# A hybrid attention and recurrence backbone: three kinds of work that surround the projections are moved, and the two edge query blocks of each head are scored in 512 columns

## The reference, cut to what matters

```python
for l in range(DEPTH):                                   # DEPTH = 2
    sh1, sc1, g1, sh2, sc2, g2 = adaln(c, mod_w[l], mod_b[l])   # silu(c) @ mod_w[l] + mod_b[l], six vectors
    n_lat = modulate(rmsnorm(h, norm1_g[l]), sh1, sc1)
    if even:  # one projection: q, k, v, xr, gr = split(n_lat @ w_in); the context gives k, v, xr too
        y = concat(neighbourhood_attention(q, k, v, kc, vc, rpb), bidir_rglru(...) * gelu(gr)) @ w_out
    else:
        y = short_conv_mixer(n_lat, o_w_in[o], o_conv_w[o], o_w_out[o])
    h = h + g1 * y
    h = h + g2 * swiglu(modulate(rmsnorm(h, norm2_g[l]), sh2, sc2), ffn_w_gu[l], ffn_w_down[l])
return rmsnorm(h, final_g)
```

## Time and profile before

| what | value |
|---|---|
| time, median of 3 runs | 2314.98 us (2313.59 to 2317.13) |
| the profiled execution's own time | 2308.03 us |
| its span, first to last instruction | 2306.2 us |
| mean granted TensorE clock | 0.992 |
| PE busy | 2241.3 us, 97% |
| DVE busy | 1480.3 us, 64% |
| POOL busy | 1143.6 us, 50% |
| ACT busy | 839.7 us, 36% |
| DMA queue q1 (SP's), q10 (ACT's) | 257.61 MB and 21.50 MB |

### The profile page before, as it was taken

How to read it: one execution, slowest core, us unless ns; L and a number is a source line. 1 busy time by engine, 2 the same in 40 slices (tenths; PEclk the granted TensorE clock), 3 DMA queues, 4 the chain that set the end, 5 groups by cost and what they waited for, 6 DMA issues and landing times.

```text
span 2306.2 us, 27368 instructions
## 1 busy us (share of the span) xinstructions
PE 2241.3 (97%) x10278; PEld 1830.8 (79%) x10278; DVE 1480.3 (64%) x1895; ACT 839.7 (36%) x1395; POOL 1143.6 (50%) x729
## 2 busy tenths in 40 slices
PE   8999999989999999999999999999999999999998
PEld 3788887878778888888888778888788888888887
DVE  5677755853786555557776987765976555555553
ACT  4544545852533333332122622234433333332112
POOL 3223313788646555556353445574356555565340
PEclk9999999999999999999999999999999999999999
DMA  9655657744222222248653122250222222242321
GB/s 339 208 151 169 188 154 189 163 134 123 61 86 88 84 85 86 84 133 284 222 194 112 32 82 82 74 186 29 60 86 85 83 85 84 83 160 96 110 81 75
DMA packets 296943, 282.95 MB, mean 123 GB/s; under 512 B 64784, under 2 KB 242156, under 8 KB 296300
## 3 DMA queue, kind: packets, MB, share of 16 engines
q1 hardware_dynamic: 258747, 257.61, 36.0%
q10 hardware_dynamic: 37488, 21.50, 3.2%
q0 software_dynamic: 576, 2.10, 0.2%
HBM read 226.36 MB, written 57.16 MB: 123 GB/s over the span
## 4 chain that ended last, share of the span: by engine, by line
PE 68%; DVE 6%; POOL 2%; issue 1%; ACT 1%; DMA 1%; DVEq 0%; POOLq 0%; ACTq 0%
PE bank L1103 22%; PE bank L1105 22%; PE bank L1104 22%; DVE act_lo L2115 1%; DMA pair_raw<-in_ffn_w_gu 1%; DVE act_hi L2115 1%; POOL slot_lo L1064 1%; POOL slot L1064 1%; DVE x_rms L2107 0%; DVE pair_raw L2092 0%; PE bank L1138 0%; DMA pair_raw<-in_o_w_in 0%; DVE bank L2026 0%; DVE t_sum L2082 0%; DVE pair_raw L2085 0%
## 5 line engine op out<-in xcount | busy, mean ns | idle before, releaser
L2034 DVE SCALAR_TENSOR_TENSOR h<-bank,mods,h 128x512 f32<-128x512 f32 x384 | 287.7, 750 | 271.5 <-PE bank L1105 266.3
L1064 POOL TENSOR_TENSOR slot_lo<-pair_raw,slot_hi 128x512 fp32r<-128x512 f32 x112 | 170.5, 1522 | 293.7 <-ACT slot_hi L1601 293.7
L1064 POOL TENSOR_TENSOR slot<-pair_raw,slot 128x512 fp32r<-128x512 f32 x144 | 234.2, 1647 | 17.3 <-ACT slot L1601 17.3
L1064 POOL TENSOR_TENSOR slot_lo<-t_sum,slot_hi 128x512 fp32r<-128x512 f32 x109 | 162.7, 1514 | 146.3 <-ACT slot_hi L1601 146.3
L2195 DVE TENSOR_TENSOR bank<-bank,p 128x512 f32<-128x512 f32 x53 | 37.0, 698 | 284.5 <-PE bank L1105 284.4
L1601 ACT CAST slot_hi<-pair_raw 128x512 fp32r<-128x512 f32 x112 | 69.0, 616 | 301.6 <-DMA pair_raw<-in_ffn_w_gu 244.2
L1103 PE MATMUL bank<-act_lo,slot_hi 128*128 128x512 f32 x436 | 171.2, 393 | 6.5 <-DVE act_lo L2115 5.9
L1103 PE MATMUL bank<-a,slot_hi 128*128 128x512 f32 x436 | 171.8, 394 | 2.6 <-ACT p L1610 0.8
L1105 PE MATMUL bank<-a,slot_hi 128*128 128x512 f32 x436 | 170.5, 391 | 0.0
L1105 PE MATMUL bank<-act_lo,slot_hi 128*128 128x512 f32 x436 | 170.2, 390 | 0.0
L1104 PE MATMUL bank<-act_lo,slot_lo 128*128 128x512 f32 x436 | 170.2, 390 | 0.0
(11 more groups left out here) (320 smaller groups left out, 5985.8 us busy)
## 6 DMA issues: line engine op xcount, KB each, us to landing
pair_raw<-in_ffn_w_gu SPq DMA_DIRECT2D x88, 512.0 KB, 4.6
mod_in_f<-in_mod_w SPq DMA_DIRECT2D x48, 512.0 KB, 3.8
z_spill<-silu_g SPq DMA_DIRECT2D x88, 256.0 KB, 2.2
mod_in_p<-in_mod_w SPq DMA_DIRECT2D x32, 512.0 KB, 6.0
pair_raw<-in_o_w_in SPq DMA_DIRECT2D x24, 512.0 KB, 3.8
raw<-in_e_w_in SPq DMA_DIRECT2D x20, 512.0 KB, 5.2
low_f<-z_spill SPq DMA_DIRECT2D x40, 256.0 KB, 4.9
a_f<-z_spill SPq DMA_DIRECT2D x18, 512.0 KB, 5.8
```

The costliest lines, as they stand in the source:

```text
L1064: nc.gpsimd.tensor_tensor(low, from_, high, ALU.subtract).then_inc(s_wlo, 1)
L2034: V.scalar_tensor_tensor(out=dst, in0=bank[:, b, :], scalar=mods[:, gate, m:m + 1], in1=dst, op0=ALU.mult, op1=ALU.add).then_inc(s_hup, 1)
```

## The change

The edge blocks of a head (kind 0 and 1, the first and the last) have two key tiles and so 256 window and 256 context keys. They are now scored by two matmuls of 512 columns into bank 0 instead of four of 256 columns across banks 0 and 1; the bias tile, the source of `logits` and the order in `turn_probs` follow. The fills of the bias move ahead of the gate weights' loads, the widening and placing one round forward, four slice loads a round move behind the bias. The totals of vector i-2 are made one by one inside group 0 of `project_in(i)` (and for the third vector inside the second V tile). DVE adds the last four slices of a vector after `gate_low(i + 1)`. The last block of y is scaled by DVE, copied by ACT and subtracted by DVE.

```diff
@@ sync
             for j in range(2):
                 load_unit(4 + j, j, column_unit(w_in, P + order_p[j]))
+            fill_bias()
             sp.wait_ge(s_gwz, 1)
...
                 load_unit(4 * i + 2, 0, column_unit(w_in, i * P + order_p[2]))
-                if i >= 2:
+                load_unit(4 * i + 3, 1, column_unit(w_in, i * P + order_p[3]))
+                if i == 1:
+                    widen_bias()
+                else:
+                    place_bias(range(ROWS // 2 * (i - 2), ROWS // 2 * (i - 1)))
                     for k in range(4):
                         load_mod_p(i - 1, k)
-                load_unit(4 * i + 3, 1, column_unit(w_in, i * P + order_p[3]))
-                if i == 1:
-                    fill_bias()
-                elif i == 2:
-                    widen_bias()
-                else:
-                    place_bias(range(ROWS // 2))
...
-                    place_bias(range(ROWS // 2, ROWS))
-                if j == 2:
-                    for k in range(4):
-                        load_mod_p(LT - 1, k)
-            for k in range(4, FT):
+            for k in range(FT):
                 load_mod_p(LT - 1, k)
@@ gpsimd (far_rows is now filled at the start)
             def out_weight(j):
+                if j == 3:
+                    pool.wait_ge(s_yf, BLOCKS)
...
             for g in range(BLOCKS):
-                y_ready(g)
+                if g < BLOCKS - 1:
+                    y_ready(g)
+                if g == BLOCKS - 2:
+                    pool.sem_inc(s_preset, 1)
@@ tensor
+            def mod_total(n, acc, m):
+                if m == 0:
+                    pe.wait_ge(s_macc, 8 * n + 10)
+                mm = pe.matmul(bank[:, 7, m:m + 1], acc[:, m * P:(m + 1) * P], ones[:, 0:1], start=True, stop=True)
+                if m == FT - 1:
+                    mm.then_inc(s_mfin, 1)
... in project_in
+                    if i >= 2 and g == 0:
+                        pe.wait_ge(s_gatev, 12 * i + 3)
+                        totals = {k: (lambda k=k: mod_total(i - 2, mod_acc_p, k)) for k in range(FT)}
-                    if i and g == 9:
-                        pe.wait_ge(s_gatev, 12 * i + 3)
-                        mod_totals(i - 1, mod_acc_p)
... in scores
+                if kind(b) < 2:
+                    step = k0 // CTX
+                    both = [k.rearrange("p (a n) -> p a n", n=CTX)[:, 0:step + 1:step, :] for k in (kh, kl)]
+                    out_ = bank_f[:, 0:HALF].rearrange("p (a n) -> p a n", n=CTX)
+                    pe.matmul(out_, q, both[0], start=True, stop=False)
+                    mm = pe.matmul(out_, q, both[1], start=False, stop=True)
@@ scalar, after the attention
+            act.wait_ge(s_yf, BLOCKS)
+            nc.scalar.copy(block_of(BLOCKS - 1, act_hi), block_of(BLOCKS - 1, y_f)).then_inc(s_yh, 1)
@@ vector
... in recur
+                if i:
+                    mod_set(i - 1, i + 1)
                 for k in range(4):
                     mod_part(i, k)
...
-                for k in range(4, FT):
-                    mod_part(i, k)
...
                     gate_low(i + 1)
-                mod_set(i, i + 2)
+                for k in range(4, FT):
+                    mod_part(i, k)
... after the attention
+            dve.wait_ge(s_preset, 4)
+            dve.wait_ge(s_fold, BLOCKS)
+            dve.wait_ge(s_invr, BLOCKS)
+            V.tensor_tensor(last_y, last_y, inv_rows[...], ALU.mult).then_inc(s_yf, 1)
+            dve.wait_ge(s_yh, BLOCKS)
+            V.tensor_tensor(block_of(BLOCKS - 1, act_lo), last_y, block_of(BLOCKS - 1, act_hi), ALU.subtract).then_inc(s_yl, 1)
```

More of the change, by code:

```diff
@@ L707, in load_bias @@
                 for j, (_, w) in enumerate(KINDS):
-                    at_ = KIND_AT[j] + CTX * j
+                    at_ = KIND_AT[j] + CTX * j + (CTX if j < 2 else 0)
                     sp.dma_start(bias_t[:, head % 2, at_:at_ + ROWS * w],
@@ L928, in _ @@
             nc.gpsimd.memset(ones[:], 1.0).then_inc(s_ident, 1)
+            nc.gpsimd.memset(far_rows[:], FAR).then_inc(s_far, 1)
             pool.wait_ge(s_rpb, 16)
@@ L1239, in project_in @@
                     pe.wait_ge(s_projev, 10 * i + g + 1)
+                    totals = None
+                    if i >= 2 and g == 0:
+                        pe.wait_ge(s_gatev, 12 * i + 3)
+                        totals = {k: (lambda k=k: mod_total(i - 2, mod_acc_p, k)) for k in range(FT)}
                     if part == 2:
@@ L1242, in project_in @@
                     else:
-                        mm = columns(bank[:, g % 5, :], unit, act_hi, proj_lo, slice(part * HALF, (part + 1) * HALF), part)
+                        mm = columns(bank[:, g % 5, :], unit, act_hi, proj_lo, slice(part * HALF, (part + 1) * HALF), part, totals)
                     mm.then_inc(s_proj, 1)
-                    if i and g == 9:
-                        pe.wait_ge(s_gatev, 12 * i + 3)
-                        mod_totals(i - 1, mod_acc_p)
             def gates(i):
@@ L1254, in gates @@
                     lo, w, low = GATE_CHUNKS[g % 3]
-                    if i and g == 2:
-                        pe.wait_ge(s_mset, i)
+                    if i >= 2 and g == 2:
+                        pe.wait_ge(s_mset, i - 1)
                     pe.wait_ge(s_gatev, 12 * i + g + 1)
@@ L1273, in _ @@
                         pe.wait_ge(s_split, U_V + k // 2 + 1)
+                    if n == 1:
+                        if k == 0:
+                            pe.wait_ge(s_gatev, 12 * LT + 3)
+                        mod_total(LT - 2, mod_acc_p, k)
                     w_hi, w_lo = w_slot(k // 2)
@@ L1279, in _ @@
                 if n == V_TILES - 3:
-                    pe.wait_ge(s_gatev, 3 + 12 * LT)
+                    pe.wait_ge(s_mset, LT - 1)
                     mod_totals(LT - 1, mod_acc_p)
@@ L1295, in scores @@
                 k0 = CTX + P * key_tiles(b)[0]
-                for out_, part in ((bank_f[:, HALF - n:HALF], slice(k0, k0 + n)), (bank_f[:, HALF:HALF + CTX], slice(0, CTX))):
-                    pe.matmul(out_, q, kh[:, part], start=True, stop=False)
-                    mm = pe.matmul(out_, q, kl[:, part], start=False, stop=True)
+                if kind(b) < 2:
[4 more added lines that the diff above has]
+                    mm = pe.matmul(out_, q, both[1], start=False, stop=True)
+                else:
+                    for out_, part in ((bank_f[:, HALF - n:HALF], slice(k0, k0 + n)), (bank_f[:, HALF:HALF + CTX], slice(0, CTX))):
+                        pe.matmul(out_, q, kh[:, part], start=True, stop=False)
+                        mm = pe.matmul(out_, q, kl[:, part], start=False, stop=True)
                 mm.then_inc(s_sc, 1)
@@ L1307, in turn_probs @@
                     pe.wait_ge(s_ptl, s - 1)
-                turned = {x: p[:, n + x * P:n + (x + 1) * P] for x in range(CT)}
+                ctx_at, win_at = (0, CTX) if kind(b) < 2 else (n, 0)
+                turned = {x: p[:, ctx_at + x * P:ctx_at + (x + 1) * P] for x in range(CT)}
                 for i, tile in enumerate(key_tiles(b)):
-                    turned[slot_of(tile)] = p[:, i * P:(i + 1) * P]
+                    turned[slot_of(tile)] = p[:, win_at + i * P:win_at + (i + 1) * P]
                 for to in sorted(turned):
@@ L2473, in _ @@
                     gate_low(i + 1)
-                mod_set(i, i + 2)
+                for k in range(4, FT):
+                    mod_part(i, k)
+            mod_set(LT - 1, LT + 1)
             dve.wait_ge(s_mset, LT)
@@ L2493, in logits @@
                 at0 = KIND_AT[kind(b)] + CTX * kind(b)
-                V.tensor_tensor_reduce(out=probs[s % 3][:, 0:w + CTX], in0=bank_f[:, HALF - w:HALF + CTX],
+                V.tensor_tensor_reduce(out=probs[s % 3][:, 0:w + CTX], in0=bank_f[:, 0:HALF] if kind(b) < 2 else bank_f[:, HALF - w:HALF + CTX],
                                        in1=bias_t[:, hd % 2, at0:at0 + w + CTX], scale=1.0, scalar=FAR, op0=ALU.add, op1=ALU.min,
```

5 lines of the change are left out of this document (3 added, 2 removed).

## The result

The changed kernel takes 2296.33 us (median of 5 runs, 2293.68 to 2297.45), the kernel before, in runs of the same comparison, 2313.59 us (5 runs, 2307.35 to 2317.13). The ratio is 0.9924, 95% interval 0.9909 to 0.9940: 17.6 us faster, between 14 and 21. A second comparison gave 0.9930 (0.9918 to 0.9942), -16.2 us. The forecast was 2305.9 us, 9.1 us faster, with a range from 2300.5 to 2315: right in its sign and outside its range. Profile against profile the difference is 2308.03 - 2295.41 = 12.6 us, so two things are to be explained: why the traces show 12.6 where 9.1 was forecast, and why the medians show some 4 us more than the traces.

A forecast was written before the change was run, and what follows sets the result against it. PE was taken as the bound (busy 97%), idle mainly at gate starts and the last y. Gaps -12.3, gates -2.4, totals +5.4, bank 7 +2.2, clock +0.8, last y -2.8: -9.1 us, 2305.9 us, range 2300.5 to 2315.

The forecast's parts named there:

- Loads and gaps: At the four gate starts: with slices and fills moved, stores of q land sooner and the gaps close, -12.3 us.
- the waits for q_spill: Sign, ACT waiting for stores of q: down from 7 to 8 us to 3 to 5.
- the share in round 1: Sign: DMA share in round 1's windows clearly under 1; staying at 1 would mean (a) or (b).
- (a): Rival: stores of q still land as late, the 12.3 us gap stays; +5.6 us, 2320.6 us; chance 7%.
- (b): Rival: the early store window closes, the late one does not; -1.9 us, 2313.1 us; chance 22%.
- Gates: Gates of each round: 8.4 instead of 9.07 us once the gap is gone, -2.4 us over four rounds.
- Totals and bank 7: Totals in group 0 and V no longer hidden, +5.4 us; first totals of rounds 2 and 3 await bank 7, +2.2 us.
- Last y: End of attention: last y moved to DVE, its subtract waiting for POOL's w_lo; PE goes on earlier, -2.8 us.
- Rival (c): DVE is not held up by POOL at the last y: -6.5 us there, 2302.2 us in all; chance 12%.
- Clock: Lower PE clock after the two pauses for bank 7: +0.8 us, from 0 to 2.
- The base: The -9.1 us was applied to the profiled 2308.03 us (2298.9) and alike to the median 2314.98 us (2305.9).

The follow-up runs named there:

- combined: Changed kernel with totals begun at the third product, bias widening and placing ahead of each round's third weight, output weight 2 made by ACT and DVE: 2292.51 us.
- weight_last: Changed kernel with POOL's weight 3 waiting for DVE's subtract of the last y instead of the multiply: 2297.09 us.
- few_totals: Changed kernel with seven of eight totals left out in three sets (21 in all), the one left at group 0's last product: 2291.31 us.
- late_totals: Changed kernel with the totals of rounds 2 and 3 begun at the third of group 0's eight products, not the first: 2295.33 us.
- behind_weight: Changed kernel with one more DVE operation ahead of the multiply of the last y, so that it comes behind POOL's weight: 2300.71 us.
- before_again: The kernel before the change, unedited, run and profiled a second time: 2312.32 us, ratio 0.9996.
- before: The kernel without the change, first profile: 2308.03 us in the profiled execution, 2313.59 us median.
- after_again: The changed kernel, unedited, run and profiled a second time: 2296.88 us.
- after: The changed kernel, first profile: 2295.41 us in the profiled execution, 2296.33 us median.

## Why the prediction was right in its sign and wrong in its size

- **Loads and gaps.** Right: -11.4 of -12.3 us, with 0.9 us left in round 0, where the margin had been put at 1 us. In round 1 xc_lo ends 1.2 us ahead of the projection (167.5 and 168.7 us), where the margin had been put at 2.5. The way there was half right: the waits for q_spill fell to 5.6 us in round 1 and to 7.7 and 5.3 in round 0, and not to 3 to 5, and the share in round 1 did not fall under 1, which the forecast had named as the sign of (a) or (b). Neither rival came: the gaps closed with the share at 1. A share of 1 says that the engines are busy, not how long a store waits behind the rest. Under 1 it went only where the bias step was gone as well (round 3, combined).
- **Gates.** -3.5 for -2.4: 8.6 us in round 0, 7.8 to 7.9 in the others, where 8.4 was taken from a range with 7.4 at its end. The shorter time comes where PE runs into the gates without a pause (7.8 in combined's round 0, which has no gap, 8.6 in weight_last's, which has 0.6 us), rounds 1 and 2 of few_totals excepted.
- **Totals and bank 7.** 5.7 for 5.4, 0.98 us twice for 1.1 twice; few_totals and late_totals confirm both. No lower clock follows the pauses of 0.98 us, which were charged with 0.8: no run shows that term, and behind these pauses the clock is 1.00.
- **Last y: the step that failed.** The forecast had "the multiply ends at 509.86 + 0.65", that is behind POOL's w_hi. It took from the earlier trace rows that DVE waits for the POOL instruction in progress, which behind_weight and the 1.62 us of the subtract bear out, and then let POOL's instruction be the one in progress. POOL sends the signal itself and starts w_hi 0.24 us behind its act_lo, DVE 0.09 us behind it; DVE was first, the subtract met w_hi and not w_lo, and PE idled 1.2 us in all where the forecast had 3. That the term was taken at -2.8 and not -5.8 is 3.0 of the 3.5 us by which the traces differ from the forecast: 1.9 of idle and 1.1 of clock. behind_weight, in which DVE does come second, takes 2300.7 us, 4.4 more than the changed kernel. Rival (c) gave nearly this term (-6.5), for a reason that is not so: DVE is held up by POOL, once and not twice.
- **Clock.** The forecast charged a lower clock behind bank 7, where none came, and left it out where the traces have it: behind the pause at the last y (0.64 before, 1.00 after, 1.1 us of the term) and behind gaps 0 to 2 (0.63 in round 0 before, 1.00 after; the gates of rounds 0 to 2 took 9.0 us before, those of round 3 8.6, but in before_again, with a clock of 0.57 in round 0, 8.7, so its price there is not settled). In behind_weight it costs 2.7 us (4.4 less 1.8 of idle).
- **The base, the other step that failed.** The forecast set the profile's difference off against the median as it stood ("7 us above that execution"), as if the 7 us had nothing to do with what the change removes. This is worth 3.6 to 5.0 us, more than the last y. In part it is traced: in the mean of the profiles the order is worth 8.2 us and not 7.2, and the +1.6 us ahead of round 0's gates is chance (+0.2 between the means of the same profiles). 12.6 + 1.0 + 1.4 = 15.0 us, beside 16.2 and 17.6 measured, with intervals that begin at 13 and 14. The granted clock (0.992 in the profiled execution, 0.990 in the median one) points the same way. What is left lies inside the intervals, and its cause stays open.

## What to carry to other kernels

When an edit hands work from POOL to DVE and the operands of both are in SBUF, work out to the tenth of a microsecond who starts first after the signal: the later one waited here until the other's instruction was over. A wait that varies with DMA traffic is to be read from several profiles before its removal is priced; here one of the shortest runs showed the least of it. And a pause of 2 to 3 us or more on PE can cost the slower products behind it as well (1.1 us behind 5.87 us in before, 2.7 behind 2.93 in behind_weight).

## What the runs showed of the hardware that was not expected

A granted clock of 1.2 GHz can follow a pause that at another time leaves it at 2.4: after PE's wait of 2.3 us for pt_lo late in the attention the next 4 us had a clock of 0.57 in after_again and 1.00 in after.

```profile
464.50:468.50 4.00, 3.93 (x16) 3.53 (x17) 2.22 (x4) 3.41 (x7) 3.06 (x3) 0.57 0.05 15
```

```profile
463.30:467.30 4.00, 3.93 (x24) 3.50 (x25) 3.53 (x7) 3.73 (x8) 3.06 (x3) 1.00 0.02 6
```

From POOL's eleventh multiply of y to its twelfth this makes 10.1 to 10.4 instead of 8.8 us, in 7 of 14 profiles, with no edit near it. The pauses of 0.98 us at bank 7 never did it (clock 1.00 behind them in after), nor did the 0.90 us at round 0's gates there.

A DVE operation held up by POOL ends 0.55 us after POOL's does in the three cases shown (alone it takes 0.69 us): the wait is the rest of POOL's instruction, whole. The Trainium skill ("SBUF — State Buffer", "SBUF: two separate sides") has such a pair, a DVE instruction with two SBUF inputs and a GpSimd one that reads SBUF, excluding each other for the whole instruction, whichever starts first; the 2.29, 2.07 and 1.62 us here agree, and POOL's w_lo, longer by 0.3 us where the subtract came between, shows that it holds in the other direction.
